# Reordering the hand-over from the first norm to the experts: the eighth tile's norm and turn move ahead, the routing choices behind them, and two weight loads ahead of the slot list

## What is computed

```python
mix = token_mixer(x, ...)                    # ends in merged @ w_out
x = layer_norm(ALPHA * x + mix, ln1_g, ln1_b)
# moe_ffn(x):
scores = sigmoid(x @ router_w.T)             # 64 experts
... group-limited choice of TOP_K = 6 experts per token, normalised gates
order = argsort(e_flat); counts = bincount(e_flat); padded = blocks of MOE_BLK = 128 rows
y_rows = for each block: (silu(h @ wg[e]) * (h @ wu[e])) @ wd[e]
shared = (silu(x @ sh_wg) * (x @ sh_wu)) @ sh_wd
x = layer_norm(ALPHA * x + routed + shared, ln2_g, ln2_b)
```

## Time and profile before

| | us |
|---|---|
| median of 3 timed runs | 2013.85 |
| the runs | 2011.6, 2013.85, 2080.27 |
| time of the profiled execution | 2022.36 |
| its span | 2020.5 |
| mean granted TensorE clock | 0.992 |
| PE busy | 1961.8 |
| the stage of the change | about 1120 to 1200 |

### The profile page before, as it was taken

One profiled execution on the slowest core, in us unless ns is written; L12 is line 12 of the kernel. 1 busy time (PEld: TensorE's weight loads), 2 busy tenths in 40 slices (PEclk: granted clock), 3 DMA queues, 4 the chain that ended last, 5 costly groups with the idle time before them and its releaser, 6 DMA issues. The chain is left out here.

```text
span 2020.5 us, 32323 instructions
## 1 busy us (share of the span) xinstructions
PE 1961.8 (97%) x9421; PEld 1478.5 (73%) x9422; DVE 1348.7 (67%) x2554; ACT 928.7 (46%) x1614; POOL 630.5 (31%) x406
## 2 busy tenths in 40 slices
PE   8999999999999999999999989999999999999996
PEld 7887787877768766668878647777777777677772
DVE  2794643444206777779877748787777887788767
ACT  2111221234212244441034247777777777677763
POOL 2443232323322220002142633333333333243334
PEclk9999999999999999999999999999999999999998
DMA  6122312122532210047770577999999999999976
GB/s 204 42 72 87 104 42 63 43 86 63 132 86 83 79 58 27 22 147 247 247 283 32 199 266 238 310 377 344 333 349 314 358 330 328 325 322 333 337 210 212
DMA packets 170898, 390.66 MB, mean 193 GB/s; under 512 B 27936, under 2 KB 100929, under 8 KB 146112
## 3 DMA queue, kind: packets, MB, share of 16 engines
q1 hardware_dynamic: 132464, 304.28, 41.7%
q0 software_dynamic: 29136, 68.52, 13.6%
q10 hardware_dynamic: 9216, 16.78, 2.2%
HBM read 338.58 MB, written 81.84 MB: 208 GB/s over the span
## 5 line engine op out<-in xcount | busy, mean ns | idle before, releaser
L649 PE MATMUL a_bank<-x_hi,w_hi 128*128 128x512 f32 x928 | 373.2, 402 | 0.0
L649 PE MATMUL a_bank<-x_hi,w_lo 128*128 128x512 f32 x928 | 362.6, 391 | 0.0
L649 PE MATMUL a_bank<-x_lo,w_hi 128*128 128x512 f32 x928 | 361.7, 390 | 0.0
L2352 DVE TENSOR_TENSOR u_lo<-w_gu,u_hi 128x1024 fp32r<-128x1024 f32 x225 | 268.1, 1219 | 37.3 <-ACT u_hi L1993 29.2
L584 POOL CAST w_hi<-w_raw 128x1024 fp32r<-128x1024 f32 x56 | 65.5, 1170 | 560.0 <-PE a_bank L649 560.0
L1993 ACT ACTIVATE u_hi<-w_gu 128x1024 fp32r x225 | 230.6, 1065 | 19.6 <-SPq L1487 19.0
L2367 DVE TENSOR_TENSOR d_lo<-w_d,d_hi 128x1024 fp32r<-128x1024 f32 x150 | 177.1, 1222 | 82.7 <-ACT d_hi L2101 81.4
L1783 PE MATMUL e_bank<-u_hi,x_g_hi 128*128 128x512 f32 x450 | 207.6, 461 | 0.0
L649 PEld LDWEIGHTS a_bank<-x_hi,w_hi 128*128 128x128 f32 x928 | 174.5, 188 | 40.8 <-issue 6.1
L649 PEld LDWEIGHTS a_bank<-x_hi,w_lo 128*128 128x128 f32 x928 | 174.3, 188 | 37.8
L649 PEld LDWEIGHTS a_bank<-x_lo,w_hi 128*128 128x128 f32 x928 | 174.7, 188 | 33.9 <-issue 0.5
(11 more groups left out here) (396 smaller groups left out, 3691.4 us busy)
## 6 DMA issues: line engine op xcount, KB each, us to landing
w_gu<-in_moe_wg SPq DMA_DIRECT2D x64, 1024.0 KB
w_gu<-in_moe_wu SPq DMA_DIRECT2D x64, 1024.0 KB
w_d<-in_moe_wd SPq DMA_DIRECT2D x64, 1024.0 KB
w_raw<-in_w_in SPq DMA_DIRECT2D x53, 512.0 KB, 3.8
gates<-gate_out ACTq DMA_DIRECT2D x64, 256.0 KB, 2.0
g_sb<-gates SPq DMA_DIRECT2D x16, 1024.0 KB, 5.3
acc_odd<-zero POOLq DMA_DIRECT2D x9, 512.0 KB, 15.0
work<-in_w_out SPq DMA_DIRECT2D x4, 1024.0 KB, 8.5
```

The source lines that it names most:

```text
L649: ins = pe.matmul(bank[h][:, :], w[:, c % 2, k, :], x[:, k, cols], start=(k == 0 and j == 0), stop=(k == KD - 1 and j == 2))
L2352: dve.tensor_tensor(up_part(u_lo[j]), up_weights(slot, j), up_part(u_hi[j]).bitcast(F32), ALU.subtract).then_inc(u_lo_dve, 1)
```

## The change

Only orders change, no work is added or removed. PE: the turn of tile 7 follows that of tile 6 at once; `counts(4)` goes between the second and third of the 8 steps of `shared_up(0)`; the counts of tiles 5 to 7 and the routers move to places between or within the shared products (6 steps, a count, 2 steps). DVE: `normed1(7)` comes before `chosen(4)` and `put(4)`; then choices and puts alternate, and `shared_sum(0)` goes behind the chain that works out the blocks. ACT: the root for tile 7 comes before the copy of turned tile 6; the copy of turned tile 7 comes before the sigmoid of tile 6. SP: `load_down(2, 2)` and `load_down(3, 3)`, 1 MB each, go ahead of the first store of `s_acc` and of the read of the slot table; they wait for the fourth `shared_up`.

```diff
             load_up(3, 3)
+            sp.wait_ge(s_gu_done, NU)
+            load_down(2, 2)
+            load_down(3, 3)
             for t in range(NU):
-                if t == 2:
-                    sp.wait_ge(s_gu_done, NU)
-                    load_down(2, 2)
-                    load_down(3, 3)
...
-            counts(NT - 4)
+            turn_x1(NT - 1)
             pe.wait_ge(e_in, EARLY_LOADS)
             pe.wait_ge(s_gu_in, 32)
             pe.wait_ge(pre_read, NT - 1)
-            shared_up(0)
+            shared_up(0, range(0, 2))
+            counts(NT - 4)
+            shared_up(0, range(2, KD))
             router(NT - 2)
-            turn_x1(NT - 1)
-            shared_up(1, 0)
             counts(NT - 3)
             router(NT - 1)
-            shared_up(1, 1)
+            shared_up(1, range(0, 6))
             counts(NT - 2)
-            shared_up(2, 0)
+            shared_up(1, range(6, KD))
             shared_turn(0)
-            shared_up(2, 1)
+            shared_up(2, range(0, 6))
+            counts(NT - 1)
+            shared_up(2, range(6, KD))
             shared_down(0)
-            counts(NT - 1)
             shared_turn(1)
...
-                if t:
+                if 0 < t < NT - 1:
                     x1_turned(t - 1)
...
+            x1_turned(NT - 2)
             scored_rows(NT - 3)
+            x1_turned(NT - 1)
             scored_rows(NT - 2)
-            x1_turned(NT - 1)
             scored_rows(NT - 1)
...
-                if t >= 3:
+                if 3 <= t < NT - 1:
                     put(t - 3)
-                if t >= 2:
+                if 2 <= t < NT - 2:
                     chosen(t - 2)
...
+            chosen(NT - 4)
+            put(NT - 4)
+            chosen(NT - 3)
+            put(NT - 3)
             chosen(NT - 2)
-            put(NT - 3)
             shared_hidden(0)
+            put(NT - 2)
             chosen(NT - 1)
-            put(NT - 2)
             shared_hidden(1)
             put(NT - 1)
             shared_hidden(2)
-            shared_sum(0)
...
+            shared_sum(0)
             dve.wait_ge(tab_done, 1)
```

More of the change, by code:

```diff
@@ L1729, in rows_out, with shared_up @@
                 ins.then_inc(mix_done, 1)
-            def shared_up(t, part=None):
+            def shared_up(t, ks=range(KD)):
                 s = t % 2
-                if t >= 2 and part != 1:
+                if t >= 2 and 0 in ks:
                     pe.wait_ge(s_silu, t - 1)
-                for k in range(KD) if part is None else range(4 * part, 4 * part + 4):
+                for k in ks:
                     ins = pe.matmul(bank[s][:, :], turned_x1(t)[:, k, :], (s_gu if t <= NU else tail_gu)[:, k, :], start=k == 0,
                                     stop=k == KD - 1)
-                if part != 0:
+                if KD - 1 in ks:
                     ins.then_inc(s_gu_done, 1)
```

## The result

The changed kernel is slower. Its median is 2024.88 us (8 runs) against 2016.51 us (8 runs) for the kernel before on the same chips; the ratio is 1.0046, 95% interval 1.0034 to 1.0057, that is +9.3 us (6.9 to 11.5). On some chips one to three executions in ten take 2070 us and more whatever the kernel; they count in the medians and are left out of all ratios. The sign is the one forecast, the size nearly three times the +3.3 us, and 2024.88 lies outside the range. Of the 7.9 us between it and the forecast of 2017, 2.7 are the base: the forecast stood on the median of 3 runs, 2013.85, which is 2016.51 with 8.

What follows compares the result with a forecast made beforehand. PE was taken as the bound, busy 1961.8 of 2020.5 us. With punctual signals, +1.6 and +1.7 made +3.3 us on 2013.85, rounded to 2017, clock and store taken as 0; range 2010.5 to 2021.5.

Steps and rivals of the forecast that it cites:

- PE as the bound, and the shift carried over: PE is busy 1961.8 of 2020.5 us; a shift of the expert loop's start reaches the end one for one.
- Late signals: Before the loop, PE's signals arrive 5.9 and 8.4 us late, at least partly from profiling; if late, +4.6 to +6.0 us.
- the punctual sum: The sum with PE's signals on time, trusted more for timed runs: +3.3 us.
- The turn ahead of the product, +1.6: PE stands until the norm of tile 7 is done before the first shared product: +1.6 us with punctual signals.
- the small waits, +1.7: Short PE waits at counts and routers within the shared products: +1.7 us with punctual signals.
- The clock, taken as 0 of 0 to 3.0: PE's clock falling to 1.2 GHz after the longer pause before the first shared product: 0 to +3.0 us, taken as 0.
- The store behind the loads, taken as 0 of 0 to 1.5: ACT waits for the first store, queued behind the loads, before scaling the third row: 0 to +1.5 us, taken as 0.
- Clock and store: Rival: the longer pause costs 3.0 us of clock and the store up to 1.5; +7 us, time 2021, chance 0.12.
- The list: The slot list, queued behind the 2 MB of loads, lands near 1182 or 1183, ahead of PE's need.
- The 2 us gained on the scatters: POOL's scatters complete the list at 1173.6 instead of 1175.5, of no value unless PE is there.
- The gather: At the loop's start, flight falls from 10.07 to about 5 us, landing near 1188 or 1189, hidden by some 6.
- the rival with the gather last: In timed runs the gather lands after PE, so the change pays; 2.7 us gain at 6 us late, 2011, chance 0.18.

Runs made afterwards that it cites:

- e16: The kernel before with four of eight steps of the fifth shared product put in PE's two pauses, loads in their old place; 2018.39 us, ratio 1.0005.
- e15: The kernel before with the two weight loads moved behind the first gathers; 2013.51 us, ratio 0.9988 against before.
- e4: The changed kernel with three more fp32 matmuls filling PE's pause ahead of the last turn; 2022.07 us, ratio 1.0039 against before.
- e3: The changed kernel with the two weight loads back behind the second store; 2018.67 us, ratio 1.0027 against before.
- e2: The kernel before with only the two weight loads moved ahead of the first store and the slot-table read; 2019.29 us, ratio 1.0031.
- e13: The kernel before with only the two weight loads moved ahead of the first store and slot-table read, run again; 2017.96 us, ratio 1.0006.
- e5: The changed kernel with the two loads between the first store and the slot-table read; 2028.35 us, ratio 1.0049 against before.
- e10: The changed kernel with the two loads between first store and slot-table read, run again; 2032.57 us, ratio 1.0045 against before.
- e14: The kernel before with the two loads between the first store and the slot-table read; 2016.21 us, ratio 1.0005.
- e1: The kernel before, no edit, profiled and timed again; 2013.56 us, ratio 1.0007.
- e9: The changed kernel itself, measured again on another chip; 2032.61 us, ratio 1.0053 against before.
- e12: The kernel before with four steps of the fifth shared product in PE's pauses and the loads behind the first gathers, second run; 2019.02 us, ratio 0.9980.

## Why the prediction was right in sign and wrong in size

**PE as the bound, and the shift carried over.** Right. The first turn after the change has no wait. In the 17 profiles (all but e16's) the first expert product starts anywhere from 1188.9 to 1213.6 us, and from there to the end it takes 817.4 to 822.0 us in each, so a later start is paid to within a few us. That neither end can be moved alone for a gain, called the centre of the forecast, isn't borne out for the gather: e15 moves it alone and is 2.4 us faster.

**Late signals.** The lateness was real, but "at least partly a cost of being profiled" was wrong. The second profile of before had none of it; on two other chips the timed runs of before took 2022 to 2023 us and the profiles there showed it again. It goes with a chip or an execution. The choice of the punctual sum was right: the norm was forecast to end at 1134.3 from a put ending at 1128.6 and took 1126.90 to 1132.59, 5.69 us for the 5.65 of the working.

**The turn ahead of the product, +1.6, and the small waits, +1.7.** Near in the total, by luck in the parts. The stretch up to the fourth product grew by 5.52 us, and with the clock's part taken off (0.9 on the turn, 1.7 on four records, both against the same work at full clock) some 2.9 remain for the 3.3. But 2.3 of them are PE's pause alone (3.17 against 0.85), where 1.6 was booked; the working had left out that the count, 0.5 us of work, no longer stands in that pause. The small waits were 0.6 at most, not 1.7: no count waited, and even at full clock (e4) the first of them waited 0.47.

**The clock, taken as 0 of 0 to 3.0.** This is the first term that failed. I set it nearer to pauses of 1.3 us, while the pause I had worked out was 3.2 us. The granted clock was at 1.2 GHz from before 1132 to 1138, for 2.6 us of loss, and once more after the second pause, 1.53 us. In e4, with the pause filled, the clock stayed up and 1.92 us of the stretch were gone. The Trainium skill (TensorE: Matmul & The Clock Gate, Part 1) has an idle PE fall back to 1.2 GHz; by that rule the upper end was due, and the trace agrees, 2.6 of the 3.0. In time the filled pause didn't separate it.

**The store behind the loads, taken as 0 of 0 to 1.5.** The second term, and in these profiles the weightier one. I named the wait and its place, with the 2.55 us ACT waits for the second store in the earlier trace rows beside it, but took it as 0, as if the first had slack. It landed after 9.04 us, behind 2 MB, and PE's pause grew by 2.31 us; the pause then cost 1.53 us of clock, which no part of the working had. Together 3.84 us. The slack had also shrunk from the other side, which the working doesn't mention: with `shared_sum(0)` behind the chain of the blocks the store left 8.8 us later. By itself that cost nothing (e3). e2 and e13 show the pause in the old orders, e5, e10 and e14 show it gone when the store leaves first; in time only e2 shows a loss clear of noise.

**The rival that had it.** *Clock and store*, at 0.12, was the mechanism that came about. Its own terms make 3.3 + 3.0 + 1.5 = 7.8 us, not the 7 written there, and 2021.7 us, just outside the range; measured in the two profiles are 8.97, in time 9.3. So the range failed with the forecast, by leaving out the far part of a case that it had named.

**The list.** Forecast to land near 1182 or 1183; DVE got it at 1185.63, after 10.5 us from its issue, where the second profile of before needed 4.3 (1175.17 to 1179.43). The Trainium skill (DMA: Bandwidth & Descriptors, Queues, rings and completion order) states that each DMA engine consumes descriptors in ring order, though a later one may finish first; the late landing fits that order, which I had priced too low. The 2 us gained on the scatters weren't there: they ended at 1173.35 against 1173.93, counted from the turn of tile 6 0.2 us later. PE was later still, so it cost nothing, as said.

**The gather.** Before, it really ends together with PE, punctual too: it landed at 1189.77 (1180.46 + 9.31), and the first turn started at 1189.82, behind a product that ended at 1189.71. After the change it flew 5.9 us, where 5 was taken, and was hidden by 5.6, where some 6 were forecast; but it landed near 1192.6 and not 1188 or 1189, since the list came 7 us later, counted from the turn of tile 6. The rival with the gather last had its grain, as e15 gains 2.4 us by that alone.

What stays open: why PE's signals come late on some chips (or whether the recorded ends, which are modelled, come early there), why e13 lost less than e2, what e15 gains beyond its stage, and what the orders would cost with the product first and punctual signals.

## What to carry to other kernels

When two stages end together, what either loses is paid in full, while moving one of them earlier gained little here (2.4 us for the gather, nothing measurable for PE's list). Before a large transfer is moved ahead in a queue, look for each small store behind it that some engine waits for: its landing time grows, here from 3.1 us to 9.0, even where it is issued on time. And a pause of the matrix engine should be priced with the slow work that may follow it: those of 3.17 and 3.64 us cost 2.6 and 1.53 us more, most of 1.3 to 1.5 us cost nothing, and one of 1.49 us was followed by 1.7 us of loss (e1).

## What was not expected of the hardware

Completion signals of PE reached other engines up to 8.4 us after the recorded work, and in e9 DVE began 5.7 us after a count, while PE's own records ran on. It is there in the first profile of before and in all eight of e5 to e12, and in none of the changed kernel's first one, e1 to e4 and e13 to e15. The two chips of e5 to e12 are those on which one kernel takes some 8 us longer (2013.9 and 2022.3 us); that the late signals make these 8 us is inferred, not shown, though in the first profile of before the loop starts 8.1 us later than in e1. In the old orders PE has other work meanwhile; in the new ones it waits for what DVE makes of the late signal, 5.2 us in e5 and e9.
